# Where the gating, the stationary taps and the stacked copies of a depthwise convolution stand in their engines' queues

## What is computed

```python
def _conv_module(x, buf, w_pw1, b_pw1, w_dw, b_dw, ln_g, ln_b, w_pw2, b_pw2):
    a, g = jnp.split(x @ w_pw1 + b_pw1, 2, axis=-1)
    u = a * jax.nn.sigmoid(g)
    c, new_buf = _causal_dwconv(u, buf, w_dw, b_dw)
    c = jax.nn.silu(_layer_norm(c, ln_g, ln_b))
    return c @ w_pw2 + b_pw2, new_buf
```

## Time and profile before

| | |
|---|---|
| median of 3 runs | 3186.91 us (3183.22 to 3187.72) |
| the profiled execution | 3185.13 us |
| its span, first to last instruction | 3183.4 us |
| mean granted TensorE clock | 0.986 of full speed |
| TensorE, VectorE, ScalarE, GpSimd busy | 3061.4, 1583.9, 790.5, 828.7 us |
| TensorE busy from 80 to 120, and from 280 to 360 us | 33.45 of 40, 55.89 of 80 us |

### The profile page before, as it was taken

One profiled execution on the slowest core, in us unless ns is written; L12 is line 12 of the kernel. 1 busy time (PEld: TensorE's weight loads), 2 busy tenths in 40 slices (PEclk: granted clock), 3 DMA queues, 4 the chain that ended last, 5 costly groups with the idle time before them and its releaser, 6 DMA issues.

```text
span 3183.4 us, 50120 instructions
## 1 busy us (share of the span) xinstructions
PE 3061.4 (96%) x20024; PEld 2843.8 (89%) x20024; DVE 1583.9 (50%) x2318; ACT 790.5 (25%) x1475; POOL 828.7 (26%) x523
## 2 busy tenths in 40 slices
PE   7998899999999999999989999999999999999997
PEld 7785689999999998999967878788999999999996
DVE  4777545433333345334357786878217333333335
ACT  4000533111111125111134444544006111111113
POOL 2232033333232323333201011112323232333330
PEclk9998899999999999999989999999999999999999
DMA  7465221111111102432255564747311111111111
GB/s 217 126 150 124 88 55 47 47 46 46 40 50 42 53 27 88 142 121 101 88 180 204 212 213 176 270 149 278 108 41 54 41 53 40 53 46 46 46 34 55
DMA packets 277968, 317.92 MB, mean 100 GB/s; under 512 B 25877, under 2 KB 217621, under 8 KB 276610
## 3 DMA queue, kind: packets, MB, share of 16 engines
q1 hardware_dynamic: 257577, 250.01, 25.5%
q10 hardware_dynamic: 12960, 40.04, 3.3%
q0 software_dynamic: 7296, 25.96, 2.3%
HBM read 224.63 MB, written 92.19 MB: 100 GB/s over the span
## 4 chain that ended last, share of the span: by engine, by line
PE 79%; DVE 10%; ACT 6%; issue 4%; DMA 1%; SPq 0%; POOL 0%; another core or an unknown queue 0%; DVEq 0%; ACTq 0%; POOLq 0%
PE ps L396 22%; PE ps L397 22%; PE ps L398 22%; PE ps L2056 2%; DVE CB L2477 2%; PE ps L1121 2%; PE ps L1164 1%; ACT X L479 1%; DVE CT L1558 1%; PE ps L1130 1%; PE ps L1131 1%; DVE RST L1722 1%; PE ps L1132 1%; PE ps L417 1%; DVE HT L1740 1%
## 5 line engine op out<-in xcount | busy, mean ns | idle before, releaser
L396 PE MATMUL ps<-AH,WH 128*128 128x352 f32 x3072 | 1001.2, 326 | 13.0 <-DVE U L2501 6.5
L397 PE MATMUL ps<-AL,WH 128*128 128x352 f32 x3072 | 986.6, 321 | 0.0
L398 PE MATMUL ps<-AH,WL 128*128 128x352 f32 x3072 | 985.9, 321 | 0.0
L381 POOL TENSOR_SCALAR WH<-RAW 128x1024 fp32r<-128x1024 f32 x200 | 237.0, 1185 | 1682.1 <-PEq L403 1484.8
L396 PEld LDWEIGHTS ps<-AH,WH 128*128 128x128 f32 x3072 | 578.0, 188 | 38.6 <-issue 29.4
L397 PEld LDWEIGHTS ps<-AL,WH 128*128 128x128 f32 x3072 | 579.3, 189 | 1.1 <-issue 0.2
L398 PEld LDWEIGHTS ps<-AH,WL 128*128 128x128 f32 x3072 | 577.7, 188 | 0.0
L383 POOL TENSOR_TENSOR WL<-RAW,WH 128x1024 fp32r<-128x1024 f32 x200 | 515.0, 2575 | 16.7
L396 PE MATMUL ps<-HH,WH 128*128 128x352 f32 x1536 | 498.4, 324 | 0.0
L397 PE MATMUL ps<-HL,WH 128*128 128x352 f32 x1536 | 492.3, 321 | 0.0
L398 PE MATMUL ps<-HH,WL 128*128 128x352 f32 x1536 | 492.0, 320 | 0.0
(11 more groups left out here) (317 smaller groups left out, 3399.2 us busy)
## 6 DMA issues: line engine op xcount, KB each, us to landing
RAW<-in_ffn_w SPq DMA_DIRECT2D x128, 512.0 KB, 3.6
CT<-in_state_mlstm_C SPq DMA_DIRECT2D x32, 1024.0 KB, 5.4
out_C_s<-CT SPq DMA_DIRECT2D x32, 1024.0 KB, 5.7
RAW<-in_ml_w_in SPq DMA_DIRECT2D x32, 512.0 KB, 3.9
RAW<-in_conv_w_pw SPq DMA_DIRECT2D x24, 512.0 KB, 8.0
STK<-u_scratch SPq DMA_DIRECT2D x64, 184.0 KB, 4.0
xc_scratch<-XC ACTq DMA_DIRECT2D x16, 528.0 KB, 2.7
so_scratch<-SO ACTq DMA_DIRECT2D x16, 528.0 KB, 3.8
```

Source lines behind the costliest of these rows:

```text
L381: pool.tensor_scalar(WH[:, k % 4], RAW[:, k % 2], 1.0, 0.0, ALU.mult, ALU.add).then_inc(w_hi, 1)
L396: pe.matmul(ps[:, bank, 0:CW], wh[:, k, cols], hi[:, k, cs], start=(k == 0), stop=False)
L397: pe.matmul(ps[:, bank, 0:CW], wh[:, k, cols], lo[:, k, cs], start=False, stop=False)
L398: mm = pe.matmul(ps[:, bank, 0:CW], wl[:, k, cols], hi[:, k, cs], start=False, stop=(k == nk - 1))
```

## The change

Three things move. (1) VectorE gates chunk 0 of tile f + 1 between its own taps 5 and 6 of tile f, and makes the sum of chunk 0 of tile f - 1 behind tap 8; chunks 1 and 2 follow the own taps, then TS of tile f. For tile 0 the two gatings of tile 1 stand behind taps 4 and 9. (2) For the last tiles TS(6) is built before the own taps of tile 7, and TS(7) behind the fourth of the own taps of its last chunk; gatings and sums are distributed between the taps. (3) The stacked copies of tile 7 get a room of their own, STK7, in that of AL, which is free once all products of this stage are done; SP loads all three chunks of tile 7 ahead of chunk 2 of tile 6. Two semaphores for STK7 take the place of g2_done and so_done, whose counts are carried on in g1_done (from 48) and sig_done (from 24).

```diff
+        STK7 = at("STK7", [P, NG, MW], F32, O_A + UNIT)
+        def stacked(f):
+            return STK7 if isinstance(f, int) and f == KT - 1 else STK
...
+        stk7_in = [sem("stk7_in0"), sem("stk7_in1")]
+        G2 = 6 * KT
+        SIG0 = 3 * KT
...
                 for c in range(3):
                     pe.wait_ge(xm_put, 3 * j - 2 + c)
-                    pe.wait_ge(so_done, 3 * j - 2 + c)
+                    pe.wait_ge(sig_done, SIG0 + 3 * j - 2 + c)
...
                 for c in chunks:
-                    wait(sp, tap_mm, tap_place(f - 1, c) + 1 if isinstance(f, int) and f else 3 * f + c - 2)
+                    if isinstance(f, int) and f == KT - 1:
+                        sp.wait_ge(g1_done, 6 * KT)
+                    else:
+                        wait(sp, tap_mm, tap_place(f - 1, c) + 1 if isinstance(f, int) and f else 3 * f + c - 2)
...
-                        sp.dma_start(STK[GRP * r:GRP * r + GRP, :, MOFF[c]:MOFF[c] + n],
-                                     US[s, :, lo:lo + n].rearrange("(g p) t -> p g t", p=GRP)).then_inc(stk_in[c], 16)
+                        sp.dma_start(stacked(f)[GRP * r:GRP * r + GRP, :, MOFF[c]:MOFF[c] + n],
+                                     US[s, :, lo:lo + n].rearrange("(g p) t -> p g t", p=GRP)).then_inc(stk7_in[c // 2] if isinstance(f, int) and f == KT - 1 else stk_in[c], 16)
...
             pw2_loads(0, (2, 3))
-            stack(KT - 1, 1, (0,))
+            stack(KT - 1, 1)
             stack(KT - 2, 0, (2,))
-            stack(KT - 1, 1, (1, 2))
...
-                pe.wait_ge(stk_in[c], 16 * NG * (f + 1))
+                if isinstance(f, int) and f == KT - 1:
+                    pe.wait_ge(stk7_in[c // 2], 16 * NG * (1 if c == 2 else 2))
+                else:
+                    pe.wait_ge(stk_in[c], 16 * NG * (f + 1))
...
+            def rows_ready(f, c):
+                dve.wait_ge(glu_done, 3 * f + c + 1)
+                if c == 2:
+                    dve.wait_ge(hist_put, f + 1)
+
+            def early(f):
+
+                if f == 0:
+                    return {4: lambda: (free_rows(1), gated(1, 1, 0)), 9: lambda: gated(1, 1, 1)}
+                return {5: lambda: (free_rows(f + 1), gated(f + 1, (f + 1) % 2, 0)), 8: lambda: tap_sums(f - 1, 0)}
+            free_rows(0)
+            for c in range(3):
+                gated(0, 0, c)
+            tap_rows()
+            dve.wait_ge(s_zero, 2)
+            dve.wait_ge(x_pre, KT + 16)
             for f in range(KT - 1):
                 s = f % 2
-                free_rows(f)
-                for c in range(3):
-                    gated(f, s, c)
-                    if f >= 2:
-                        tap_sums(f - 2, c)
-                if f == 0:
-                    tap_rows()
-                    dve.wait_ge(s_zero, 2)
-                    dve.wait_ge(x_pre, KT + 16)
-                else:
-                    tap_stationary(f - 1, 1 - s)
-                dve.wait_ge(glu_done, 3 * f + 3)
-                dve.wait_ge(hist_put, f + 1)
-                own_taps(f, s, tile_taps * f, 0, TOK)
+                rows_ready(f, 2)
+                own_taps(f, s, tile_taps * f, 0, TOK, early(f))
+                if f == KT - 2:
+                    break
+                for c in range(1, 3):
+                    if f or c == 2:
+                        gated(f + 1, 1 - s, c)
+                    if f:
+                        tap_sums(f - 1, c)
+                tap_stationary(f, s)
             f, s = KT - 1, (KT - 1) % 2
-            base = tile_taps * f
-            free_rows(f)
-            for c in range(2):
-                gated(f, s, c)
-                tap_sums(f - 2, c)
-                dve.wait_ge(glu_done, 3 * f + c + 1)
-                base = last_own[c] = own_taps(f, s, base, c * CW, c * CW + CW)
             tap_stationary(f - 1, 1 - s)
-            gated(f, s, 2)
-            dve.wait_ge(glu_done, 3 * f + 3)
-            dve.wait_ge(hist_put, f + 1)
-            last_own[2] = own_taps(f, s, base, 2 * CW, TOK, {4: lambda: tap_sums(KT - 2, 0), 8: lambda: tap_sums(KT - 3, 2)})
-            tap_stationary(f, s)
-            for n in range(2, 5):
-                tap_sums(*TAIL[n])
+            gated(f, s, 1)
+            rows_ready(f, 0)
+            base = last_own[0] = own_taps(f, s, tile_taps * f, 0, CW)
+            tap_sums(f - 2, 1)
+            rows_ready(f, 1)
+            base = last_own[1] = own_taps(f, s, base, CW, 2 * CW, {6: lambda: gated(f, s, 2)})
+            tap_sums(f - 1, 0)
+            rows_ready(f, 2)
+            last_own[2] = own_taps(f, s, base, 2 * CW, TOK, {3: lambda: (tap_stationary(f, s), tap_sums(f - 2, 2)), 8: lambda: tap_sums(f - 1, 1)})
+            tap_sums(*TAIL[3])
+            tap_sums(*TAIL[4])
```

More of the change, by code:

```diff
@@ L154, in program @@
         STK = at("STK", [P, NG, MW], F32, O_X)
+        STK7 = at("STK7", [P, NG, MW], F32, O_A + UNIT)
+        assert NG * MW * 4 <= 6 * TOK * 4
+        def stacked(f):
+            return STK7 if isinstance(f, int) and f == KT - 1 else STK
         WT = at("WT", [P, KT, NG, NQ], F32, O_X + NG * MW * 4)
@@ L289, in program @@
         e_keep = sem("e_keep")
-        g2_done = sem("g2_done")
+        G2 = 6 * KT
         acc2 = sem("acc2")
@@ L294, in program @@
         s_wif, g_w, setup_steps = sem("s_wif"), sem("g_w"), sem("setup_steps")
-        ma_mm, xm_put, so_done, km_done = sem("ma_mm"), sem("xm_put"), sem("so_done"), sem("km_done")
+        ma_mm, xm_put, km_done = sem("ma_mm"), sem("xm_put"), sem("km_done")
+        SIG0 = 3 * KT
         gate_mm, gs_put, ge_ev, mtaps, sgx_done, xc_done = sem("gate_mm"), sem("gs_put"), sem("ge_ev"), sem("mtaps"), sem("sgx_done"), sem("xc_done")
@@ L788, in first_pair_pe @@
                     pe.wait_ge(xm_put, 2 * n - 5)
-                    pe.wait_ge(so_done, 2 * n - 5)
+                    pe.wait_ge(sig_done, SIG0 + 2 * n - 5)
                 for h in range(2):
@@ L822, in spill_tile @@
             wait(act, xc_done, j + 1)
-            wait(act, so_done, 3 * j + 3)
+            act.wait_ge(sig_done, SIG0 + 3 * j + 3)
             act.dma_start(XCS[j], XC[:, s]).then_inc(spill[s], 16)
@@ L841, in a_out @@
             act.wait_ge(ma_mm, n + 2)
-            act.activation(SO[:, s, ch[c]], ps[:, bank + 1, 0:CW], ACT.Sigmoid).then_inc(so_done, 1)
+            act.activation(SO[:, s, ch[c]], ps[:, bank + 1, 0:CW], ACT.Sigmoid).then_inc(sig_done, 1)
         def keep_rows(act, j, s, count):
@@ L2055, in tap_products @@
                         x0 = MOFF[c] + NG * q
-                        mm = pe.matmul(out[:, 0:w], taps, STK[:, g, x0:x0 + w], start=(q == 0), stop=(c < 2 and q == NQ - 1), skip_group_check=True)
+                        mm = pe.matmul(out[:, 0:w], taps, stacked(f)[:, g, x0:x0 + w], start=(q == 0), stop=(c < 2 and q == NQ - 1), skip_group_check=True)
                     for g in range(NG if c == 2 else 0):
@@ L2059, in tap_products @@
                         taps = TS[:, s, NQ * g + q]
-                        ud = STK[:, g, MDEC:].rearrange("p (b w) -> p b w", w=HIST + DEC_T)[:, :, NG * q:NG * q + DEC_T]
+                        ud = stacked(f)[:, g, MDEC:].rearrange("p (b w) -> p b w", w=HIST + DEC_T)[:, :, NG * q:NG * q + DEC_T]
                         mm = pe.matmul(out[:, w:CW], taps, ud, start=False, stop=(q == NQ - 1), skip_group_check=True)
@@ L2133, in pw2 @@
                         pe.wait_ge(w_split, 16 + 2 * u + h + 1)
-                    release = (g2_done, 2 * i, 2) if h == 0 and i and (c == 2 and u % 2 or c == 0 and u == 2) else None
+                    release = (g1_done, G2 + 2 * i, 2) if h == 0 and i and (c == 2 and u % 2 or c == 0 and u == 2) else None
                     aside = second_half if u == 0 and h == 0 else None
-                    product(pe, bank_of(c, u, h), (2 * u + h) % 4, P, 0, AH, AL, KT, ch[c], release, aside).then_inc(g2_done, 1)
+                    product(pe, bank_of(c, u, h), (2 * u + h) % 4, P, 0, AH, AL, KT, ch[c], release, aside).then_inc(g1_done, 1)
                     if h == 0 and between:
@@ L2146, in _ @@
             ln_pe(pe, ln_m0, lambda c, u, between: pw2(c, 2 + u, between), 2, acc2, 12)
-            free_panels(pe, g2_done, 24, 2)
+            free_panels(pe, g1_done, G2 + 24, 2)
             ffn_pe(pe, 0, 0, True, False, before=(acc2, 24))
@@ L2157, in _ @@
             pe.wait_ge(xm_put, 3 * NJ)
-            pe.wait_ge(so_done, 3 * NJ)
+            pe.wait_ge(sig_done, SIG0 + 3 * NJ)
             for j in range(NJ):
@@ L2574, in add2 @@
                 for h in range(2):
-                    dve.wait_ge(g2_done, 2 * i + h + 1)
+                    dve.wait_ge(g1_done, G2 + 2 * i + h + 1)
                     x = X[:, 2 * u + h, ch[c]]
```

## The result

| | before | after |
|---|---|---|
| median | 3186.44 us (5 runs, 3183.22 to 3187.72) | 3169.64 us (5 runs, 3165.85 to 3171.71) |
| the profiled execution | 3185.13 us | 3167.34 us |
| its span | 3183.4 us | 3165.6 us |
| mean granted TensorE clock | 0.986 | 0.990 |

The ratio is 0.9947, 95% interval 0.9932 to 0.9961: faster by 16.8 us. The forecast was 3171 us, range 3166 to 3179.

The account below looks back on a forecast made before the run. TensorE, busy 96% of the span, was taken as the bound, so only its waits on VectorE mattered. 7.5 + 7.7 = 15.2 us off 3185.13 gave 3169.9, about 3171 for the median; range 3166 to 3179.

Parts of the forecast that it names:

- the two stalls: TensorE's waits: 6.55 us for tile 1's gating, and 7.9 us for tile 6's tap matrix in the last tiles.
- Part 1: Tile 0: gating tile 1 between VectorE's own taps removes TensorE's first stall; gain 7.5 us, 6.6 to 8.2.
- Part 2: Tiles in between, up to 285.3 us: moved gatings and sums cost 0, up to 0.5 us in tile 6.
- Part 3: Last two tiles: VectorE's reordered queue takes 50.5 to 51.6 us instead of 58.65; gain 7.7 us.
- what I left to the range, up to 1.5: Last two tiles: TensorE's taps, at half clock after the new stall, could take back up to 1.5 us.
- The new stall: TensorE would wait about 6 us before tile 6's chunk 1 taps, for VectorE's sum of tile 6 chunk 0.
- Part 4: SP's load queue and tile 7's own room: 0, with up to 2 us loss if tile 6's chunk 2 lands slowly.
- Part 5: Merged semaphores may add register additions per wait in the mLSTM input loop: 0, at most 2 us loss.
- a stretch I took as unchanged in length: Layer norm and second pointwise product after the last tiles: order unedited, so an earlier start moves the whole rest.
- The rule on the shared port: Last tiles: no own taps pass during GpSimd's split, 7.7 us lost instead of 4.8 to 5.9; not adopted.
- only the first stall goes: Rival: late sum or loads in the last two tiles leave part 3 only 0 to 3; 3176 to 3179, 12%.
- Only the last part goes: Rival: tile 2's products wait for panels or tap matrix, part 1 falls to 2 or less; 3177, 6%.

Follow-up runs that it names:

- Experiment 1: Kernel before with only tile 1's first two gatings moved behind own taps 4 and 9 of tile 0; 3178.4 us, ratio 0.9971.
- experiment 2: Changed kernel with VectorE's old order in the last two tiles, keeping STK7 and SP's new order; 3177.84 us, ratio 0.9971.
- experiment 4: Changed kernel with VectorE's old order of gatings and sums in tiles 1 to 5; 3168.67 us, ratio 0.9943.
- experiment 5: Changed kernel with TensorE releasing tile 7's panels only behind the mean part of chunk 0, so GpSimd splits them later; 3174.24 us, ratio 0.9956.
- Experiment 3: Changed kernel without STK7: tile 7's stacked copies go into STK again, in SP's old load order; 3170.41 us, ratio 0.9949.
- experiment 6: Changed kernel with tile 7's panels released behind the mean part and SP loading tile 6 chunk 2 ahead of tile 7 chunk 2; 3164.42 us, ratio 0.9927.
- experiment 9: Changed kernel with tile 1's first gating behind own tap 8 of tile 0 instead of tap 4; 3175.92 us, ratio 0.9967.

## Why the prediction was right

The forecast for the median was 1.4 us above what came. The mechanism was right in both halves: the two stalls went where they were said to go, and each time for the reason given. The sum was close in part by compensation: the parts brought 14.5 us of the 15.2 forecast, and 3.0 us came from where none was forecast.

- **Part 1, 7.5 us:** 7.4 to 7.8. No idle time near 83, taps(0, 0) at 91.22 where 91.5 stood, gate(1, 0) at 77.29 plus 0.57, i.e. 77.9, where 78.3 stood; TS(0) was held by 0.7 us by the split, inside the 1.6 allowed. Experiment 1, which has this part alone, gained 8.0, experiment 2 (with SP's new order and that of the middle tiles) 8.6.
- **Part 2, 0:** shown by experiment 4.
- **Part 3, 7.7 us:** 7.1. The queue was added up well (51.51 us where 50.5 to 51.6 stood) and the split cost 5.2 us where 4.8 to 5.9 stood. Part of what I left to the range, up to 1.5, came as 0.71 us: TensorE's taps behind the stall took 8.99 us for the pair instead of 6.3 and held sum(7, 0). The new stall is 7.84 us, not some 6: sum(6, 0) came at 290.98, a microsecond later than reckoned, and taps(5, 2) were done at 283.7.
- **Part 4, 0:** right in the sum, and the step under it was the weakest. I had stack(6, 2) land near 296 from a median landing of 4.0 us; it landed at 302.3, with 0.1 to 0.2 us in hand. That row has the 64 loads of chunks 0 and 1, of 184 KB. The loads of chunk 2 are 310 KB, and stand in rows of their own in the view of DMAs, one for each of a chunk's four loads; the first and the last, in the changed kernel:

```profile
STK<-u_scratch SPq DMA_DIRECT2D x8, 311.0 KB, 4.1
STK<-u_scratch SPq DMA_DIRECT2D x8, 309.5 KB, 7.0
```

  The kernel before has 3.8 and 6.8 us there, so each load takes 1.0 us longer to land than the one ahead of it, and the eighth of a row would take 3.8 + 7 x 1.0 = 10.8 us by this estimate. It took 10.6. The row to price it was there. The need at 302 was right; in experiment 5, where the need came at 297, the miss cost a wait of 6.0 us. Experiment 3 shows no worth of the room and SP's new order.
- **Part 5, 0:** not tried by itself, but the mLSTM stage lies behind the second pointwise product, and from there to the end pass 2831.1 us against 2831.0 (2831.1 to 2832.5 in the experiments). The 0.05 us per wait in the prediction's bound was a guess, and no run has a price for such an addition.
- **Not forecast: 3.0 us** in a stretch I took as unchanged in length. The view by stretches (length; busy us and count of TensorE, its weight loads, VectorE, ScalarE, GpSimd; granted clock; DMA share; GB/s) for 40 us behind the stall, after and then before:

```profile
310.00:350.00 40.00, 30.25 (x252) 21.11 (x253) 22.29 (x14) 28.95 (x33) 0.00 (x0) 0.87 0.42 142
```

```profile
325.00:365.00 40.00, 30.17 (x234) 18.95 (x235) 21.14 (x13) 26.11 (x29) 0.00 (x0) 0.79 0.50 159
```

The granted clock was 0.87 and 0.79. The partial sums of the layer norm show it group by group, 16 matmuls each, after and then before:

```profile
312.91 1.39 PE L424 MATMUL ps<-SQ,ones_g 128*32 128x352 f32 x16 [3.34 <-ACT SQ L460]
314.11 1.37 PE L424 MATMUL ps<-CB,ones_g 128*32 128x352 f32 x16
323.23 1.39 PE L424 MATMUL ps<-SQ,ones_g 128*32 128x352 f32 x16 [2.90 <-ACT SQ L460]
326.31 2.25 PE L424 MATMUL ps<-CB,ones_g 128*32 128x352 f32 x16
```

```profile
327.81 1.91 PE L417 MATMUL ps<-SQ,ones_g 128*32 128x352 f32 x16 [3.35 <-ACT SQ L453]
329.47 2.59 PE L417 MATMUL ps<-CB,ones_g 128*32 128x352 f32 x16
339.82 2.58 PE L417 MATMUL ps<-SQ,ones_g 128*32 128x352 f32 x16 [2.90 <-ACT SQ L453]
344.18 2.08 PE L417 MATMUL ps<-CB,ones_g 128*32 128x352 f32 x16
```

6.4 us against 9.2, a difference of 2.8. The same stretch measured 36.2 us in experiments 1, 2 and 6, 34.1 in 3, 35.5 in 4 and 34.0 in 9, which have the same TensorE instructions there (in 4 and 9 with a wait for a load). The groups alone do not give its length: in experiment 9 they take 5.5 us.

  Every run has its mean granted clock on record, and runs of one kernel differ in it. Experiment 1 had 0.987 in four of seven runs, 3178.4 to 3180.8 us, and 0.989 or 0.990 in the other three, 3174.3 to 3175.4 us. The five runs of experiment 5 part in the same way: 0.990 in the two short ones, 0.988 or 0.989 in the others. So one and the same kernel can take some 4 us less in a run with the higher mean clock. The kernel before had 0.985 to 0.987 in all 31 runs beside the experiments; the changed kernel 0.988 to 0.991 in its five, the slowest at 0.988 and the fastest at 0.991. A part of the 3 us therefore seems to come with the change, by way of the clock, and a part to be the luck of the profiled execution, which is 2.3 us below its median. How it divides stays open: by the medians the order of the last tiles is worth 8.2 (experiment 2 less the changed kernel) where VectorE's queue gives 7.1, but 1 us is less than such a difference can tell. The four runs of experiment 1 at 0.987 lie 7.2 us below the kernel before, near the 7.4 of the timeline.

**The rule on the shared port.** I weighed the Trainium skill, "SBUF — State Buffer", section "Who interferes with whom", by which a VectorE instruction with two SBUF inputs and a GpSimd one that reads SBUF exclude each other, and went by the rows. I had it as "nothing passes while the split runs", and that reading was wrong: the section speaks of single instructions, and a split is four of them. Seen one by one, the four pieces begin at 283.42, 284.66, 287.24 and 288.51 and take 1.20, 2.54, 1.24 and 2.54 us, 0.61 each when alone. GpSimd's four instructions end at 284.26, 286.82, 288.10 and 290.67. Each piece ends 0.3 to 0.4 us after one of them: one piece passes per GpSimd instruction. In this the trace agrees with the section. In experiment 5 the four pieces alone take 2.44 us, and GpSimd's split alone (at 296.06, VectorE idle) 1.05 + 2.34 + 1.05 + 2.34 = 6.8. One after the other, without overlap, both would need 9.2 us; in the changed kernel both were through between 283.21 and 291.05, 7.8 us. So the lengths in the profile overlap by 1.4 us in all, and adding them up gives too high a price. Which part of an instruction's length is exclusive no run shows, and lengths on GpSimd are rough in the profile. The loss was 5.2 us, where my reading of the rule gave 7.7.

Of the rivals, "only the first stall goes" is what experiments 1 and 2 build, and both lie at 3178, where 3176 to 3179 stood. "Only the last part goes" was not built; with the 8.2 us that the last tiles are worth on top of the first stall, it would lie near 3178 too, if the parts add that way round.

## What to carry to other kernels

Where one engine's queue feeds another, put the instruction that the other waits for between the pieces of the long work, and price the wait with what comes behind it: here 3.8 us of waiting cost 6. Ask of every release what it sets going and on whom it falls: a split that GpSimd did at the earliest moment cost 5 us of the very taps that TensorE waited for, and holding it back won 5 to 8 us on top of the change's 16.8, once the loads were in the order of need. Before speeding up what stands ahead of a load, look how much time the load has in hand (0.1 to 0.2 us here), and price it from the row of its own size; loads ordered by need, not by tile, made 9.8 us of difference between two kernels that were alike otherwise. And before explaining a few microseconds between two traces, compare the granted clock of all runs.

## What the runs showed of the hardware

- A short idle time of TensorE costs more than itself: 3.83 us idle, then 5.7 us of products at the lower of its two clocks (0.49 us instead of 0.32 for 352 columns in the profile, 0.29 instead of 0.16 from start to start). With 6.55 us idle the slow stretch was 3.4 us. Each is one execution.
- With products in one idle time, what followed directly ran at full clock (3.17 us per 40 taps), but not what followed the next long wait, of 2.16 us.
- The mean granted clock of the same kernel differs between runs: in experiment 1 it was 0.987 or 0.989 to 0.990, and the runs of the second kind were some 4 us shorter.
- Loads of one queue land in a row: the eight STK loads issued from 277.6 to 280.8 us (184 KB each) landed 0.5 to 1.2 us apart, the last 5.8 us after its issue; the eight issued from 288.5 to 291.7 (chunk 2 of both tiles, 310 KB each) 1.3 to 1.5 us apart, the last 10.6 us after. In experiment 6 the loads of chunk 2 were 1.3 to 1.7 apart. The larger loads land further apart; whether their size alone does it was not tried.
- A VectorE instruction with two SBUF inputs beside GpSimd's split: four pieces took 1.20, 2.54, 1.24 and 2.54 us instead of 0.61 each, and each ended 0.3 to 0.4 us after one of GpSimd's four instructions. The two engines' work, 9.2 us when each is alone, took 7.8.
